# The last expert of each expert phase: up loaded in two parts, down in four, with TensorE's products following part by part

## The reference

```python
def expert_block(args):
    xblk, e = args
    return (jax.nn.silu(xblk @ w_gate[e]) * (xblk @ w_up[e])) @ w_down[e]

yb = lax.map(expert_block, (xb, block_exp)).reshape(n_rows, d)
return jnp.zeros((n_tok + 1, d), h.dtype).at[row_tok].add(yb * row_w[:, None])[:n_tok]
...
out = hier_moe(jnp.concatenate([h2.reshape(b * s, d), hc2.reshape(-1, d)], axis=0), *moe)
x = x + g2 * out[: b * s].reshape(x.shape)
```

## Time and profile before

| | |
|---|---|
| median of 3 runs | 2225.81 us (2224.89 to 2227.06) |
| the profiled execution | 2223.05 us |
| its span in the profile | 2221.2 us |
| PE busy | 2116.6 us (95%) |
| DVE busy | 868.1 us (39%) |
| granted PE clock, mean | 0.989 |
| data moved | 628.50 MB, 283 GB/s in the mean |

### The profile page before, as it was taken

One profiled execution on the slowest core, in us unless ns is written; L12 is line 12 of the kernel. 1 busy time (PEld: TensorE's weight loads), 2 busy tenths in 40 slices (PEclk: granted clock), 3 DMA queues, 4 the chain that ended last, 5 costly groups with the idle time before them and its releaser, 6 DMA issues. The chain is left out here.

```text
span 2221.2 us, 27768 instructions
## 1 busy us (share of the span) xinstructions
PE 2116.6 (95%) x10798; PEld 1366.0 (61%) x10812; DVE 868.1 (39%) x1880; ACT 361.1 (16%) x693; POOL 81.3 (4%) x84
## 2 busy tenths in 40 slices
PE   8999999999999999999999999999999898898896
PEld 7888888868888888554554444446647443343343
DVE  3376766234666769451111111122553311111112
ACT  2321112322111131230000000012132000000001
POOL 0000000000000010000000000010000000000000
PEclk9999999999999999999999999999999999999999
DMA  8646677333576675239999999995232799999994
GB/s 292 227 180 247 216 249 280 114 114 114 211 258 249 228 254 203 83 121 374 426 427 425 425 425 427 385 402 191 76 152 114 281 423 424 425 426 426 426 394 203
DMA packets 135462, 628.50 MB, mean 283 GB/s; under 512 B 8391, under 2 KB 14567, under 8 KB 101601
## 3 DMA queue, kind: packets, MB, share of 16 engines
q1 hardware_dynamic: 123024, 595.90, 67.5%
q0 software_dynamic: 10224, 27.19, 3.5%
q10 hardware_dynamic: 2144, 4.46, 0.5%
HBM read 606.41 MB, written 30.41 MB: 287 GB/s over the span
## 5 line engine op out<-in xcount | busy, mean ns | idle before, releaser
L794 PE MATMUL T<-ring,S 128*64 128x512 f32 x2112 | 484.0, 612 | 52.5 <-DMA ring<-in_exp_w_up 50.8
L794 PEld LDWEIGHTS T<-ring,S 128*64 128x64 f32 x2112 | 151.7, 140 | 338.4 <-issue 326.1
L676 PE MATMUL T<-X,ring 128*128 128x256 f32 x1536 | 337.6, 379 | 0.7 <-ACT X L1249 0.7
L676 PEld LDWEIGHTS T<-X,ring 128*128 128x128 f32 x1536 | 290.9, 190 | 40.7 <-issue 1.6
L1610 DVE SCALAR_TENSOR_TENSOR S<-ring,cs,S 128x512 f32<-128x512 f32 x336 | 228.5, 745 | 0.0
L825 PE MATMUL T<-ring,S 128*64 128x512 f32 x976 | 219.9, 592 | 0.0
L1851 DVE TENSOR_TENSOR S<-S,T 128x256 f32<-128x256 f32 x66 | 27.8, 421 | 443.6 <-ACT S L1334 443.6
L781 PE MATMUL T<-S 128*128 128x128 f32 x1600 | 185.9, 277 | 1.2 <-DVE S L1770 1.2
L781 PEld LDWEIGHTS T<-S 128*128 128x128 f32 x1600 | 182.9, 193 | 1.4 <-DVE S L1770 1.0
L684 PE MATMUL T<-S,ring 128*128 128x256 f32 x768 | 174.8, 381 | 0.0
L684 PEld LDWEIGHTS T<-S,ring 128*128 128x128 f32 x768 | 144.9, 190 | 29.3 <-DVE S L1638 10.1
(11 more groups left out here) (326 smaller groups left out, 1716.0 us busy)
## 6 DMA issues: line engine op xcount, KB each, us to landing
ring<-in_exp_w_gate SPq DMA_DIRECT2D x66, 2048.0 KB, 15.7
ring<-in_exp_w_up SPq DMA_DIRECT2D x66, 2048.0 KB, 20.3
ring<-in_exp_w_down SPq DMA_DIRECT2D x65, 2048.0 KB, 18.5
ring<-in_ffn_w_up SPq DMA_DIRECT2D x24, 2048.0 KB, 12.6
ring<-in_mod_w SPq DMA_DIRECT2D x24, 2048.0 KB, 7.9
ring<-in_ffn_w_down SPq DMA_DIRECT2D x12, 2048.0 KB, 7.9
y_rows<-zb POOLq DMA_DIRECT2D x4, 3072.0 KB, 26.0
ring<-in_kv_w SPq DMA_DIRECT2D x4, 2048.0 KB, 15.0
```

The source lines that it names most:

```text
L676: ins = pe.matmul(T[:, m % 2, h * S:(h + 1) * S], w[:, k, m * P:(m + 1) * P], x1[:, k, :], start=(k == 0), stop=(k == KT - 1))
L794: ins = pe.matmul(T[c * B:(c + 1) * B, s, :].rearrange("p (g n) -> p g n", g=2), xgT[:, k, s * B:(s + 1) * B], w[:, :, k * CH + c * 256:k ...
```

## The change

Up of the last turn's block 1 is loaded by two DMAs of 1 MB, each with half of the k tiles and its own semaphore (`last_up` for the first half), and PE waits for the second half only before k tile 4. Down of that block is loaded by four DMAs of 512 KB, one for each f tile (`last_part` for the first three), and PE waits for each before the first of its two products. One product of block 0 instead of two comes ahead of the alternation, and six products of zeros instead of ten stand before `up`. Each down part now has one piece of 4 KB for each partition, each half of up one of 8 KB. All of this is done in both layers, and only in the last turn.

```diff
+        last_up, last_part = sem("last_up"), sems("last_part", 3)
...
                 a0, b0 = expert_of(tl, 0), expert_of(tl, 1)
-                gate_up(tl, b0)
+                sp_.wait_ge(r["m_full"], 2 * tl + 2)
+                load(3, weights[0][l][ds(b0, 1)])
+                src = weights[1][l][ds(b0, 1)].rearrange("e (p k) n -> p (e k n)", p=P)
+                for h in range(2):
+                    at = slice(h * 4 * CH, (h + 1) * 4 * CH)
+                    sp_.dma_start(ring[:, 4, at], src[:, at]).then_inc((last_up, r["landed"][4])[h], 16)
                 down(tl, 0, a0)
-                down(tl, 1, b0)
+                sp_.wait_ge(r["y_full"], 2 * tl + 2)
+                src = weights[2][l][ds(b0, 1)].rearrange("e (c p a) n -> p (e c) a n", c=2, p=P)
+                for f in range(MJ):
+                    sp_.dma_start(mslot(5, MJ, D)[:, f, :], src[:, f // 2, f % 2, :])\
+                        .then_inc((last_part + r["landed"][5:6])[f], 16)
...
-                def up(i, s, at, sems_, nth_):
-
-                    for j in range(2):
-                        pe.wait_ge(sems_[j], 16 * nth_)
+                def up(i, s, at, sems_, nth_, in_parts=False):
+
+                    pe.wait_ge(sems_[0], 16 * nth_)
+                    if in_parts:
+                        pe.wait_ge(last_up, 16 * l + 16)
+                    else:
+                        pe.wait_ge(sems_[1], 16 * nth_)
                     pe.wait_ge(r["xT"], 2 * i + (s + 2))
                     w = ring[:, at:at + 2, :]
                     for k in range(KT):
+                        if in_parts and k == 4:
+                            pe.wait_ge(sems_[1], 16 * nth_)
...
-                keep_busy(10, 3)
-                up(tl, 1, 3, second, tl + 1)
+                keep_busy(6, 3)
+                up(tl, 1, 3, second, tl + 1, in_parts=True)
...
-                for f, n in order[0:2]:
-                    last_down(0, f, n)
-                pe.wait_ge(r["landed"][5], 16 * tl + 16)
+                last_down(0, *order[0])
                 pe.wait_ge(r["hT"], 2 * tl + 2)
                 for j in range(8):
-                    if j + 2 < 8:
-                        last_down(0, *order[j + 2])
+                    if j + 1 < 8:
+                        last_down(0, *order[j + 1])
+                    if j in (0, 2, 4):
+                        pe.wait_ge(last_part[j // 2], 16 * l + 16)
+                    if j == 6:
+                        pe.wait_ge(r["landed"][5], 16 * tl + 16)
                     last_down(1, *order[j])
```

## The result

The changed kernel takes 2229.41 us in the median of 15 runs (2224.64 to 2231.57), the kernel before 2225.81 us in 15 (2222.32 to 2228.88). The ratio is 1.0015, with a 95% interval of 1.0008 to 1.0021: 3.6 us slower, within 0.2%. The prediction was 2229.2.

The account below looks back on a forecast made before the run. Gathered rows, not weights, were taken to gate the end of layer 0, and both ends after the change. Layer 0's +1.8 us and layer 1's +1.6 made +3.4 us: 2229.2 us from 2225.81, range 2223.5 to 2231.5.

Parts of the forecast that it names:

- Up in two parts: Last turn, both layers: half of up lands ahead of the whole, so up starts 1.9 and 2.5 us earlier.
- Down in four parts: Last turn, both layers: parts land in order of use, removing stops of 0.24 and 0.73 us and 0.86 us of lone products.
- The gathers gate: Before both combines: gathers start no sooner despite PE's gain; smaller load packets delay the last one 0.3 us (0 to +1.3).
- The clock: Both combines: PE idles some 3.9 us before them, then runs one slow stretch costing 1.7 us (0 to 3.0).
- The early loads: End of layer 0: w_in_cd, issued 3.1 us sooner, shares bandwidth and delays the last gather 1.5 us (0 to 1.9).
- The sum: Both layer ends together: +1.8 us in the first, +1.6 in the second, +3.4 us in all, giving 2229.2 us.
- waits of 2.8 us and more: PE's earlier waits: four of six between 2.8 and 3.3 us, all three at 4.9, were followed by a slow stretch.

Follow-up runs that it names:

- a_early: Changed kernel with gathers reading stand-in rows from an expert's weights, not waiting for its stores (output not the reference's); 2234.32 us, 1.0038 of the kernel before.
- b_early: Kernel before with gathers reading stand-in rows from an expert's weights, not waiting for its stores (output not the reference's); 2239.71 us, 1.0065 of the kernel before.
- a_busy: Changed kernel plus 17 products of zeros between the last down product and the combine, in both layers; 2225.91 us, 1.0003 of the kernel before.
- a_hold: Changed kernel, but in layer 0 w_in_cd is issued only once all four gathered tiles are scaled; 2228.09 us, 1.0009 of the kernel before.
- second look: The changed kernel profiled once more, with no further edit; one run, 2230.12 us.
- E0: Not a run: layer 0's time from the down products of the turn before to the first sums of squares; 40.10 us before, 41.61 changed.
- down_only: Changed kernel's down in four parts alone, up as one load with ten products of zeros; 2227.77 us, 1.0008 of the kernel before; repeated (_again), one run, 2225.04 us.

## Why the prediction was right

- **Up in two parts.** Forecast to start at 1474.3 and 2174.1; in the times of before it starts at 1474.16 and 2174.26.
- **Down in four parts.** Forecast to start at 1482.7 and 2182.5 and end at 1490.6 and 2190.4; it does at 1482.80 and 2182.65, 1490.47 and 2190.48. The first part, issued at 2176.49, landed 11.5 us later at 2188.0, which is 2183.4, as forecast. The whole takes 7.67 and 7.83 us; against before that is 1.4 and 1.7 us less, where 1.1 and 1.6 were worked out.
- **The gathers gate.** Forecast: cb unchanged but for +0.3 us. Measured: -0.06 and +0.29 us, and a_early against b_early shows that PE's gain passes through once they don't gate.
- **The clock.** Forecast: one slow stretch of 1.7 us at each end. Measured by a_busy: 1.7 and 1.6 us (1.5 and 1.7 by the length of the combine alone). This is the cause of the slowdown in both layers. The low end of the range (0) was not seen behind idle time of this length: all six combines that began after 3.95 to 4.61 us of it (two profiles of the changed kernel, one of a_hold) had the slow stretch.
- **The early loads: the term of layer 0's sum that was mis-sized.** The step gave the last gather 1.5 + 0.3 us more delay, and 1.8 us to the end of layer 0 by itself. G grew by 0.66 us (0.87 in the second look), and a_busy, with the same early loads, has no loss in layer 0 at all: the term is worth nothing there. The sharing itself was sized well: in 1493 to 1496 the gathers of the changed kernel moved 0.72 MB, 240 GB/s where 224 was forecast, and from the end of POOL's last issue to the use it took 7.23 us (6.56 in the second look, 6.55 in a_busy) against 5.72 before and 4.8 to 4.9 with the loads held: 0.8 to 1.5 us more than before. What the step left out is POOL. In the kernel before its sixth and seventh issues were long, ahead of any load of w_in_cd, so that its last issue ended 10.85 us after the first; in the changed kernel it was 10.00. Before, then after:

```profile
1490.24 1.71 POOL L2221 DMA_INDIRECT ring<-y_rows,dst  x1 [0.30 <-issue]
...
1488.66 1.10 POOL L2239 DMA_INDIRECT ring<-y_rows,dst  x1 [0.30 <-issue]
```

E0's 1.5 us are the clock's. The prediction had named the clock as the term behind the gathers' and of the same size, so the sum stayed right; that the two were alike is luck, and its account of layer 0 put the wrong one in front.
- **The sum.** +1.8 and +1.6 forecast, +1.51 and +1.56 in the profile (+2.23 and +1.56 in the second look). That 2229.2 met 2229.41 so closely is partly luck: the two ends explain 3.1 of the medians' 3.6 us, and single executions differ by several us in the code between.

Left open: why POOL's last issues in layer 0 are longer in some executions (0.94 to 1.92 us), and what part of the medians' 3.6 us beyond 3.1 belongs to the change.

## What to carry to other kernels

Before a stall is cut, look for the second thing that the next stage waits for, and how late it is: here the gathered rows were ready 0.6 us behind PE's end in one layer and 0.5 us ahead of it in the other, so 3 and 4 us of faster products bought nothing. Time that an engine saves ahead of such a gate becomes idle time in one piece, and for TensorE that can cost the clock of the work behind it; some products of zeros in the gap took that back, as long as they ended before the gate opened. And ask what an earlier end releases: here the next loads, which meet the transfers that gate.

## What the hardware showed that was not expected

- Idle time of 1.96, 2.05, 2.25 and 2.51 us before PE's work was followed by a slow stretch (28 records of down in 8.78 us for 7.09; a granted clock of 0.50 in 1493.7 to 1497.1 of down_only), where I had leaned on waits of 2.8 us and more. The trace of the kernel before already had such cases, which the prediction didn't use:

```profile
1798.44 8.78 PE L794 MATMUL T<-ring,S 128*64 128x512 f32 x32 [2.01 <-DMA ring<-in_exp_w_up]
```

  The length of the idle time alone doesn't settle it: at the same place, layer 1's last up, 2.31 us before was followed by full clock and 2.32 us in down_only_again by a slow stretch.
- The twelve gathers of the two layers (6.3 MB) beside the weights of the turns ahead cost some 14 us in all (b_early against the kernel before), while the same bytes at the end of the phase are mostly hidden behind PE.
